# Mamba-2 blocks in a fused encoder step: the two products of x on GpSimd get a semaphore each, and one of them moves to an earlier step

## The chip, the cores and the metric

The kernel runs on 1 core of one Trainium2 chip. The metric is the device time of one launch in microseconds (us), median of several runs. Five engines work side by side and meet only through semaphores: TensorE (PE; its weight loads are PEld), VectorE (DVE), ScalarE (ACT), GpSimd (POOL) and SyncE (SP), which only issues DMAs. Each works through its own list of instructions in order: one that waits holds up all behind it on that engine.

## What is computed

One inference step of a two-layer encoder trunk for 512 prompt tokens and 64 sample tokens, in fp32: layer 0 mixes tokens by sliding-window attention, layer 1 by Mamba-2 (SSD); both have a cross-attention into 256 memory tokens, an output projection and a squared-ReLU MLP. The change lies in the SSD of layer 1:

```python
acs = jnp.cumsum(dtf * A, axis=2)
xdt = xf * dtf[..., None]
decay = jnp.exp(jnp.where(causal, diff, -jnp.inf))
cb = jnp.einsum('bcqgn,bcsgn->bcqsg', Cf, Bf)
y_diag = jnp.einsum('bcqsg,bcqsgh,bcsghp->bcqghp', cb, decay, xdt)
decay_end = jnp.exp(acs[:, :, -1:] - acs)
states = jnp.einsum('bcsgn,bcsgh,bcsghp->bcghpn', Bf, decay_end, xdt)
...
y_off = jnp.einsum('bcqgn,bcghpn,bcqgh->bcqghp', Cf, h_in, jnp.exp(acs))
```

x is needed twice: times dt (inner product, for y_diag) and times dt and the decay to the block's end (state product, for states). Then y is gated by silu(z) and normed by group.

## The kernel before

Activations lie transposed in SBUF, features on the partitions and 576 token columns (64 sample, 512 prompt) in the free dimension. Every weight matrix is cut into slabs of 1024 x 128; there are 242. A slab comes by DMA from SyncE into a ring of four (`raw`), ScalarE rounds it to fp32r (`w_hi`, L472), GpSimd makes the rest (`w_lo`, L1954), and TensorE multiplies in three products (L959). A slab is eight eighths of 6 matmuls each.

Layer 1 runs the eight SSM groups in pairs, one `turn` for each of the four pairs. `ssd_steps` (L144) writes a turn's order down once, and every engine walks the same list and does its own part of each step:

- K: an eighth of a slab of the projections for this pair's z and the next pair's x, B and C (80 eighths a turn; in the last turn z and the memory queries, 56). At a slab's end come `slab_end` and the conv on it: VectorE's `xp` (L1792, reads PSUM), ScalarE's first tap (L770), three taps on VectorE (L1807), tanh and silu (L784, L1814), and on GpSimd `w_lo` and two copies to `tails` (L2055).
- A(b), b = 0 to 4: block b (64 sample tokens, then four of 128) is transposed to tokens on partitions: `xtok`, `btok`, `cbm`.
- dec(b): ScalarE makes the decays (`dec`, L856 and L863) and the grown rows exp(acs) (`row`, L861) from rows that it fetched by DMA (L816, issued after an earlier diag, since the buffers alternate); VectorE masks dec (L1895); GpSimd multiplies the rows by C (L2095; not for block 1).
- st(b): TensorE makes the block's state from the state product (L1332); GpSimd decays the old state (`hbd`, in `rstd`, L2102).
- diag(b): TensorE makes y from dec and the inner product (L1345), and from the grown rows and the state (L1355). VectorE adds it to y (L1904) and makes the new state (L1913). GpSimd makes both products of x for block b + 1 (`scaled_x`, L2075 state product, L2076 inner product) into the buffer `xd`, which lies in `sq`.
- Q, G, N: gating on VectorE (L1918), squares on ScalarE (L870), their sums on TensorE (L1366, L1371), roots and norm (L1924).

Among the steps stand st(b), dec(b + 1), diag(b), st(b + 1) at equal distances, some 2.7 eighths in turns 1 to 3 and 1.3 in the last. `xd_done` counts after the inner product alone; st(b) waits for it, diag(b) doesn't.

## Time and profile before

| | |
|---|---|
| three runs | 1857.19, 1854.53, 1864.68 us (median 1857.19) |
| the profiled execution | 1860.35 us |
| its span, first to last instruction | 1858.5 us |
| TensorE busy | 1757.7 us, 95% |
| VectorE, ScalarE, GpSimd busy | 791.6, 698.7, 749.0 us |
| mean granted clock of TensorE | 0.986 |

The times of single instructions come from that one profiled execution. TensorE's clock has two levels, 1.2 and 2.4 GHz; a granted clock of 1.00 is the higher, 0.50 the lower. "A <- B" in a row means that A was released by B, or that tile A is made from tile B. The four turns lie between some 939 and 1284 us of the span.

### The profile page before, as it was taken

The numbers are of one execution on the slowest core, as the hardware profiler recorded it, in microseconds if no ns is written. First come the engines' busy times: TensorE is split into PE (matmuls) and PEld (weight loads), VectorE is DVE, ScalarE is ACT, GpSimd is POOL, SyncE is SP. The second block draws the span as 40 slices with busy tenths as digits, with TensorE's granted clock in tenths as the row PEclk, the third lists the DMA queues.
The fourth block names the chain that finished last, engine by engine and source line by source line (L and its number), as shares of the span: only waits on it lengthen the run. The fifth ranks groups of instructions, "written<-read, shape, count | busy, mean of one in ns | idle before, by whom it ended". The sixth has DMA issues, their size and how long they took to land.

```text
span 1858.5 us, 31140 instructions
## 1 busy us (share of the span) xinstructions
PE 1757.7 (95%) x13115; PEld 1683.0 (91%) x13115; DVE 791.6 (43%) x1534; ACT 698.7 (38%) x1318; POOL 749.0 (40%) x438
## 2 busy tenths in 40 slices
PE   6999999999999999999899999989999999999996
PEld 5997887998999999998798989877898999999996
DVE  5427777315412112126856676755504411212124
ACT  6416666324312121224455555553514312122221
POOL 1231121242736354451345555553232745445451
PEclk9999999999999999999899999998999999999998
DMA  5521210121222222221222222212121222222221
GB/s 217 191 80 52 69 64 30 57 87 51 91 84 87 80 80 85 86 80 46 84 88 87 78 94 83 92 60 102 46 80 58 91 80 80 86 85 80 80 87 67
DMA packets 47659, 153.68 MB, mean 83 GB/s; under 512 B 8257, under 2 KB 10017, under 8 KB 47265
## 3 DMA queue, kind: packets, MB, share of 16 engines
q1 hardware_dynamic: 40144, 140.59, 22.3%
q10 hardware_dynamic: 7376, 11.10, 1.8%
q8 instruction: 104, 1.70, 0.4%
q14 instruction: 35, 0.28, 0.0%
HBM read 145.21 MB, written 6.47 MB: 82 GB/s over the span
## 4 chain that ended last, share of the span: by engine, by line
PE 81%; DVE 8%; ACT 4%; POOL 3%; issue 2%; DMA 1%; SPq 0%; POOLq 0%; DVEq 0%; ACTq 0%
PE ps L959 70%; DVE mix L1459 1%; PE ps L942 1%; PE ps L1123 1%; PE ps L1094 1%; POOL sq L2075 1%; ACT dec L856 1%; DVE x L1462 1%; PE ps L1175 1%; PE ps L1112 1%; PE ps L1198 1%; PE ps L1332 1%; POOL w_lo L1954 1%; DVE big_lo L1403 1%; DMA raw<-in_slabs 1%
## 5 line engine op out<-in xcount | busy, mean ns | idle before, releaser
L1954 POOL TENSOR_TENSOR w_lo<-raw,w_hi 128x1024 fp32r<-128x1024 f32 x225 | 547.9, 2437 | 753.3 <-ACT w_hi L472 661.2
L959 PE MATMUL ps<-big_hi,w_hi 128*128 128x288 f32 x3552 | 781.1, 301 | 7.9 <-POOL w_lo L1954 3.2
L959 PE MATMUL ps<-big_lo,w_hi 128*128 128x288 f32 x3552 | 758.9, 297 | 7.7 <-DVE big_lo L1403 7.7
L959 PE MATMUL ps<-big_hi,w_lo 128*128 128x288 f32 x3552 | 765.1, 296 | 0.0
L959 PEld LDWEIGHTS ps<-big_hi,w_hi 128*128 128x128 f32 x3552 | 574.9, 190 | 17.6 <-issue 12.5
L959 PEld LDWEIGHTS ps<-big_lo,w_hi 128*128 128x128 f32 x3552 | 571.3, 189 | 13.1 <-DVE big_lo L1403 12.2
L959 PEld LDWEIGHTS ps<-big_hi,w_lo 128*128 128x128 f32 x3552 | 575.9, 189 | 0.1
L472 ACT ACTIVATE w_hi<-raw 128x1024 fp32r<-128x1024 f32 x242 | 255.3, 1057 | 489.7 <-DMA raw<-in_slabs 479.8
L1713 DVE TENSOR_TENSOR mix<-ps,mix 128x576 f32<-128x576 f32 x62 | 47.0, 758 | 307.3 <-PE ps L959 307.3
L1701 DVE SCALAR_TENSOR_TENSOR relu<-ps,rstd 128x576 f32<-128x576 f32 x60 | 45.4, 757 | 280.2 <-PE ps L959 280.2
L1997 POOL TENSOR_TENSOR hid<-relu 128x576 f32<-128x576 f32 x64 | 98.6, 1543 | 157.6 <-DVE relu L1701 157.5
L714 ACT ACTIVATE big_hi<-relu 128x576 fp32r<-128x576 f32 x64 | 43.9, 685 | 158.7 <-DVE relu L1701 157.0
L1807 DVE SCALAR_TENSOR_TENSOR u<-xp,par,u 128x579 f32<-128x579 f32 x84 | 93.2, 1110 | 7.5 <-ACT u L770 4.9
L1401 DVE TENSOR_TENSOR big_lo<-hid,big_hi 128x576 fp32r<-128x576 f32 x64 | 75.6, 1181 | 11.1 <-POOL hid L1997 11.1
L1439 DVE TENSOR_TENSOR sq_sum<-sq_sum,sq 128x576 f32<-128x576 f32 x20 | 15.1, 754 | 114.1 <-ACT sq L491 113.8
L1587 DVE CUSTOM_DVE_ANT_0 prob<-ps,bias,minus_sink 128x128 f32<-128x128 f32 (+2 forms) x120 | 48.4, 440 | 13.7 <-PE ps L1094 11.7
L959 PE MATMUL ps<-m_hi,w_hi 128*128 128x256 f32 x128 | 39.7, 310 | 15.2 <-POOL w_lo L1954 11.8
L2055 POOL COPY tails<-xp 128x3 f32<-128x3 f32 x56 | 17.3, 339 | 87.1 <-DVE xp L1792 82.0
L611 ACT ACTIVATE prob<-prob,stat 128x256 f32<-128x256 f32 (+2 forms) x108 | 50.4, 470 | 4.1 <-DVE stat L1587 4.0
L2095 POOL TENSOR_TENSOR row<-row,c_cur 128x768 f32<-128x768 f32 (+1 forms) x16 | 25.2, 1575 | 64.7 <-ACT row L861 64.7
L1605 DVE TENSOR_SCALAR prob<-prob,stat 128x256 f32<-128x256 f32 (+3 forms) x148 | 48.8, 366 | 3.0
L491 ACT ACTIVATE sq<-ps 128x576 f32<-128x576 f32 x14 | 9.1, 651 | 104.6 <-PE ps L959 104.6
(197 smaller groups left out, 1644.6 us busy)
## 6 DMA issues: line engine op xcount, KB each, us to landing
raw<-in_slabs SPq DMA_DIRECT2D x242, 512.0 KB, 3.4
row<-acs_prompt ACTq DMA_DIRECT2D x16, 384.0 KB, 3.3
bias<-in_alibi SPq DMA_DIRECT2D x12, 256.0 KB, 2.7
x<-in_x SPq DMA_DIRECT2D x2, 1152.0 KB, 8.6
out_h<-state ACTq DMA_DIRECT2D x4, 384.0 KB, 2.6
out_y<-x SPq DMA_DIRECT2D x2, 576.0 KB, 2.8
kms<-in_mk SPq DMA_DIRECT2D x2, 512.0 KB, 5.2
vms<-in_mv SPq DMA_DIRECT2D x2, 512.0 KB, 6.3
```

The costliest lines, as they stand in the source:

```text
L472: act.activation(w_hi[:, s % RING], raw[:, s % RING], ACT.Copy).then_inc(hi_done, 1)
L611: act.activation(ap, ap, ACT.Exp, bias=stat[:, r, 0, b:b + 1], scale=-1.0, accum_out=stat[:, r, 2, b:b + 1])
L714: act.activation(big_hi[:, m], relu[:, m % 2], ACT.Square).then_inc(act_hi, 1)
L959: ins = pe.matmul(ps[:, bank + h, 0:hi_c - lo_c], w[:, s % RING, kt], a[:, k0 + kt, lo_c:hi_c], start=start, stop=stop, skip_group_check=True)
L1401: ins = dve.tensor_tensor(dst, src, hi.bitcast(F32), ALU.subtract)
L1587: ins = dve.tensor_tensor_reduce(prob[half, r, k, c0:c1], ps[half, bank, k * 2 * P + c0:k * 2 * P + c1], bias[half, j, e, c0 + d:c1 + d], ...
L1605: ins = dve.tensor_scalar(ap, ap, stat[0:rows, r, 2, b:b + 1], None, ALU.mult)
L1701: dve.scalar_tensor_tensor(out=halves(relu[:, m % 2]), in0=src, scalar=0.0, in1=halves(rstd[:, 1]), op0=ALU.max, op1=ALU.mult).then_inc(fr ...
L1713: dve.tensor_tensor(halves(mix[:, m]), src, halves(mix[:, m]), ALU.add).then_inc(freed, 1)
L1807: dve.scalar_tensor_tensor(out=u[:, t], in0=xp[:, t % 2, j:j + UC], scalar=conv_par(gp, t)[:, j:j + 1], in1=u[:, t], op0=ALU.mult, op1=ALU ...
L1954: pool.tensor_tensor(w_lo[:, s % RING], raw[:, s % RING], w_hi[:, s % RING].bitcast(F32), ALU.subtract).then_inc(lo_done, 1)
L1997: pool.tensor_tensor(hid[:, m % 2], relu[:, m % 2], relu[:, m % 2], ALU.mult).then_inc(hid_done, 1)
```

## The change

The two products of x become steps of their own. The state product gets a semaphore `xs_done`, and GpSimd makes it in dec(b), ahead of the grown rows, as soon as st(b - 1) has released its half of the buffer. The inner product stays in diag(b - 1), now waits for diag(b - 1) alone, and keeps `xd_done`. TensorE's st(b) waits for `xs_done`, and diag(b) waits for `xd_done` as well.

```diff
                     elif kind == "st":
-                        pe.wait_ge(xd_done, at(loop, xd_done, b + 1))
+                        pe.wait_ge(xs_done, at(loop, xs_done, b + 1))
...
                     elif kind == "diag":
                         pe.wait_ge(decm_done, at(loop, decm_done, b + 1))
+                        pe.wait_ge(xd_done, at(loop, xd_done, b + 1))
...
-                def scaled_x(b):
+                def scaled_x(k, b, kind, done):
                     rows = DEC if b == 0 else P
+                    xb = xtok[0:rows, b].rearrange("p (h d) -> p h d", h=PH)
+                    pool.tensor_tensor(xd[0:rows, k], xb, wide(heads(kind, b)[0:rows], rows), ALU.mult).then_inc(done, 1)
+
+                def x_states(b):
+                    pool.wait_ge(xtok_done, at(loop, xtok_done, b + 1))
+                    need(pool, loop, st_done, b)
+                    alone(pool)
+                    scaled_x(1, b, 2, xs_done)
+
+                def x_within(b):
                     pool.wait_ge(xtok_done, at(loop, xtok_done, b + 1))
                     need(pool, loop, diag_done, b)
-                    need(pool, loop, st_done, b)
                     alone(pool)
-                    xb = xtok[0:rows, b].rearrange("p (h d) -> p h d", h=PH)
-                    pool.tensor_tensor(xd[0:rows, 1], xb, wide(heads(2, b)[0:rows], rows), ALU.mult)
-                    pool.tensor_tensor(xd[0:rows, 0], xb, wide(heads(0, b)[0:rows], rows), ALU.mult).then_inc(xd_done, 1)
+                    scaled_x(0, b, 0, xd_done)
...
                     elif kind == "A" and b == 1:
-                        scaled_x(0)
-                    elif kind == "dec" and b != 1:
+                        x_states(0)
+                        x_within(0)
+                    elif kind == "dec":
+                        if b:
+                            x_states(b)
+                        if b == 1:
+                            continue
                         pool.wait_ge(grown_done, at(loop, grown_done, later(b)))
...
                     elif kind == "diag" and b < BLOCKS - 1:
-                        scaled_x(b + 1)
+                        x_within(b + 1)
```

ScalarE also waits once a turn, at A(0), for `xs_done` beside `xd_done`.

GpSimd, turns 1 to 3, from the products for block 3 to the products for block 4, before (`sq` holds the products of x, `rstd` the decayed state, `row` the grown rows):

```order
L2075 TENSOR_TENSOR sq<-xtok,hs 128x384 [waits st_done,xtok_done,diag_done]
L2076 TENSOR_TENSOR sq<-xtok,hs 128x384
L2102 TENSOR_TENSOR rstd<-state,hs 128x384 [waits state_done]
L1954 TENSOR_TENSOR w_lo<-raw,w_hi 128x1024 [waits hi_done]
L2055 COPY tails<-xp 128x3 [waits freed]
L2055 COPY tails<-xp 128x3
L2095 TENSOR_TENSOR row_91<-row_91,c_cur 128x768 [waits grown_done,c_done]
L2075 TENSOR_TENSOR sq<-xtok,hs 128x384 [waits st_done,xtok_done,diag_done]
L2076 TENSOR_TENSOR sq<-xtok,hs 128x384
```

and after (the product that waits for st_done is the state product, the one that waits for diag_done the inner one):

```order
L2073 TENSOR_TENSOR sq<-xtok,hs 128x384 [waits xtok_done,diag_done]
L2116 TENSOR_TENSOR rstd<-state,hs 128x384 [waits state_done]
L1956 TENSOR_TENSOR w_lo<-raw,w_hi 128x1024 [waits hi_done]
L2057 COPY tails<-xp 128x3 [waits freed]
L2057 COPY tails<-xp 128x3
L2073 TENSOR_TENSOR sq<-xtok,hs 128x384 [waits xtok_done,st_done]
L2109 TENSOR_TENSOR row_91<-row_91,c_cur 128x768 [waits grown_done,c_done]
L2073 TENSOR_TENSOR sq<-xtok,hs 128x384 [waits xtok_done,diag_done]
```

The state product went from behind the grown rows to ahead of them; nothing else changed its place.

GpSimd in the last turn, from the first decayed state to the second, before:

```order
L2102 TENSOR_TENSOR rstd<-state,hs 128x384 [waits h_loaded,state_done]
L1954 TENSOR_TENSOR w_lo<-raw,w_hi 128x1024 [waits hi_done]
L2075 TENSOR_TENSOR sq<-xtok,hs 128x384 [waits st_done,xtok_done,diag_done]
L2076 TENSOR_TENSOR sq<-xtok,hs 128x384
L2095 TENSOR_TENSOR row_110<-row_110,c_cur 128x768 [waits grown_done,c_done]
L2075 TENSOR_TENSOR sq<-xtok,hs 128x384 [waits st_done,xtok_done,diag_done]
L2076 TENSOR_TENSOR sq<-xtok,hs 128x384
L2102 TENSOR_TENSOR rstd<-state,hs 128x384 [waits state_done]
```

and after:

```order
L2116 TENSOR_TENSOR rstd<-state,hs 128x384 [waits h_loaded,state_done]
L2073 TENSOR_TENSOR sq<-xtok,hs 128x384 [waits xtok_done,st_done]
L1956 TENSOR_TENSOR w_lo<-raw,w_hi 128x1024 [waits hi_done]
L2073 TENSOR_TENSOR sq<-xtok,hs 128x384 [waits xtok_done,diag_done]
L2073 TENSOR_TENSOR sq<-xtok,hs 128x384 [waits xtok_done,st_done]
L2109 TENSOR_TENSOR row_110<-row_110,c_cur 128x768 [waits grown_done,c_done]
L2073 TENSOR_TENSOR sq<-xtok,hs 128x384 [waits xtok_done,diag_done]
L2116 TENSOR_TENSOR rstd<-state,hs 128x384 [waits state_done]
```

Here the state product of block 1 also passes a whole w_lo.

## Rows read from the trace of the kernel before

**Rows 1.** The page, part 1: busy us of each engine (share of the span)

```profile
PE 1757.7 (95%) x13115; PEld 1683.0 (91%) x13115; DVE 791.6 (43%) x1534; ACT 698.7 (38%) x1318; POOL 749.0 (40%) x438
```

**Rows 2.** Table of waits, TensorE: total us, times, longest; whole run, first, last turn

```profile
PE ps L1332 <- POOL sq L2076: 26.7, 16, 3.8
...
PE ps L1288 <- DVE dts L1863: 4.9, 1, 4.9
...
PE ps L1332 <- POOL sq L2076: 6.0, 4, 2.4
...
PE ps L1332 <- POOL sq L2076: 9.3, 4, 3.8
PE ps L1345 <- DVE dec L1895: 0.9, 1, 0.9
```

**Rows 3.** Timeline of TensorE, first turn: start us, us, instruction [idle before <- releaser]

```profile
986.75 0.89 PE L1332 MATMUL ps<-sq,btok 128*128 128x192 f32 x4 [1.71 <-POOL sq L2076]
...
997.39 0.89 PE L1332 MATMUL ps<-sq,btok 128*128 128x192 f32 x4 [1.72 <-POOL sq L2076]
...
1011.73 2.10 PE L1366 MATMUL ps<-gsq,mats 128*128 128x288 f32 x8
```

**Rows 4.** Stretches: length, busy us of PE, PEld, DVE, ACT, POOL, clock, DMA

```profile
985.80:996.40 10.60, 8.91 (x76) 8.37 (x76) 6.96 (x11) 5.94 (x12) 7.88 (x8) 1.00 0.23 72
...
920.00:926.00 6.00, 6.00 (x23) 4.45 (x24) 5.66 (x7) 1.82 (x2) 2.99 (x3) 0.50 0.00 0
...
1156.00:1160.00 4.00, 4.00 (x18) 4.00 (x19) 1.49 (x4) 0.56 (x1) 3.29 (x3) 0.57 0.16 44
...
1236.00:1240.00 4.00, 3.98 (x15) 4.00 (x16) 1.21 (x1) 2.61 (x6) 1.69 (x1) 0.50 0.00 0
```

**Rows 5.** Timeline of GpSimd, the same block and what follows

```profile
986.57 0.82 POOL L2102 TENSOR_TENSOR rstd<-state,hs 128x384 f32<-128x384 f32 x1
987.36 2.40 POOL L1954 TENSOR_TENSOR w_lo<-raw,w_hi 128x1024 fp32r<-128x1024 f32 x1
...
993.26 1.69 POOL L2095 TENSOR_TENSOR row<-row,c_cur 128x768 f32<-128x768 f32 x1 [2.72 <-ACT row L861]
994.91 1.54 POOL L2075 TENSOR_TENSOR sq<-xtok,hs 128x384 f32<-128x384 f32 x1
...
1001.14 2.38 POOL L1954 TENSOR_TENSOR w_lo<-raw,w_hi 128x1024 fp32r<-128x1024 f32 x1
```

**Rows 6.** Timeline of VectorE, the same block and the turn's end

```profile
989.42 0.95 DVE L1814 SCALAR_TENSOR_TENSOR u<-th,u 128x579 f32<-128x579 f32 x1
990.45 2.55 DVE L1807 SCALAR_TENSOR_TENSOR u<-xp,par,u 128x579 f32<-128x579 f32 x3
993.93 1.83 DVE L1895 TENSOR_TENSOR dec<-dec,cbm 128x768 f32<-128x768 f32 x1 [0.93 <-ACT dec L863]
...
996.16 0.54 DVE L1913 TENSOR_TENSOR state<-rstd,ps 128x384 f32<-128x384 f32 x1
...
1001.08 4.77 DVE L1807 SCALAR_TENSOR_TENSOR u<-xp,par,u 128x579 f32<-128x579 f32 x3
...
1006.70 1.95 DVE L1918 TENSOR_TENSOR mix<-mix,zs 128x1728 f32<-128x1728 f32 x1
```

**Rows 7.** Timeline of ScalarE, the squares at the turn's end

```profile
1008.68 1.83 ACT L870 ACTIVATE gsq<-mix 128x576 f32<-128x576 f32 x3 [7.63 <-DVE mix L1918]
```

**Rows 8.** Timeline of the last turn, TensorE and ScalarE

```profile
1236.02 1.62 PE L1332 MATMUL ps<-sq,btok 128*128 128x192 f32 x4 [3.81 <-POOL sq L2076]
...
1253.17 1.62 PE L1332 MATMUL ps<-sq,btok 128*128 128x192 f32 x4 [3.52 <-POOL sq L2076]
...
1246.10 1.87 ACT L856 ACTIVATE dec<-row,hs 128x128 f32<-128x128 f32 x6 [7.46 <-DMA row<-acs_prompt]
```

**Rows 9.** The chain that ended last: 18 products at either level of the clock

```profile
954.36 2.37 PE ps L959 x18
...
1237.64 4.32 PE ps L959 x18
```

More of the change, by code:

```diff
@@ L380, in build @@
         dec_done, decm_done = sem("dec_done"), sem("decm_done")
-        xd_done, diag_done = sem("xd_done"), sem("diag_done")
+        xs_done, xd_done, diag_done = sem("xs_done"), sem("xd_done"), sem("diag_done")
         st_done, hbd_done, state_done = sem("st_done"), sem("hbd_done"), sem("state_done")
@@ L444, in build @@
                    "h_loaded": 16, "h_stored": 16}
-        for s_ in (tok_done, xtok_done, cbm_done, drop_done, dec_done, decm_done, xd_done, diag_done, st_done, state_done, y_done):
+        for s_ in (tok_done, xtok_done, cbm_done, drop_done, dec_done, decm_done, xs_done, xd_done, diag_done, st_done, state_done, y_done):
             SSM_PER[s_.name] = BLOCKS
@@ L833, in turn @@
                             need(act, loop, gsum_done, 0)
+                            need(act, loop, xs_done, 0)
                             need(act, loop, xd_done, 0)
```

## Prediction

> **What bounds the kernel now.** I read the page first: TensorE is busy for 95% of the span [rows 1], so only time in which it stands still, or runs at its lower clock, can be given back. The table of waits then names the place. TensorE's longest wait for another engine is the one the change aims at: the state product "st" (L1332) waits for GpSimd's second product of x (L2076), 26.7 us in 16 waits, of which 6.0 us lie in the first of the four turns and 9.3 us in the last [rows 2]. The second and third share the other 11.4 us.
>
> Next I read one block of the first turn engine by engine. st starts at 986.75 and again at 997.39, 1.71 and 1.72 us late [rows 3]: a block takes 10.6 us, of which TensorE works 8.9 us (8.91 us busy in that stretch, full clock) [rows 4]. GpSimd does six things in it: the decayed state (0.82), w_lo (2.40), two tiny copies (I count 0.2), the grown rows (1.69), and the two products of x, of the decayed state's size, the first in 1.54 [rows 5]. VectorE does a silu step (0.95), three taps (2.55), and the masking of dec (1.83), then y and the state [rows 6].
>
> The reader should see that these rows interlock. The masking is issued at 993.93, 0.67 us after the grown rows began, and takes 1.83 us; GpSimd's first product starts at 994.91, when the grown rows are over, and takes 1.54 us where the decayed state, as large, takes 0.82. Taken in turn, 994.95 to 995.76 is the masking and 995.76 to 996.45 the product. The same holds at the other end: the first tap at 1001.08 sits through a w_lo of 2.38 us, so that three taps need 4.77 us and not 2.55 [rows 5, 6]. Instructions of VectorE with both inputs in SBUF and GpSimd's instructions exclude each other; VectorE's reads of PSUM (y, state, xp) don't. So the two engines share one resource. Its load per block, without waits: GpSimd 0.82 + 2.40 + 0.2 + 1.69 + 0.82 + 0.82 = 6.7 us, VectorE 0.61 (989.76 to 990.37) + 2.55 + 0.82 = 4.0 us, together 10.7 us, less some 0.04 us at each of eight hand-overs: 10.4 us. The block has 10.6 us, and the one stretch in which neither works, 993.00 to 993.26, makes up the difference. **The wait at st is the visible end of a resource that is full in these blocks, not a mere matter of order.**
>
> **The change, part by part.** No instruction is added or removed, no DMA moves, no queue but GpSimd's gets another order. Three edits.
>
> (1) The wait of st. It no longer needs the grown rows, the masking and both products of x, only the state product, which now stands before the grown rows, in the 2.7 us for which GpSimd idles behind ScalarE (the wait named in the row at 993.26) [rows 5]. All 26.7 us of this wait are open to go, and with them what TensorE loses at its low clock after long waits.
>
> (2) The new wait. diag now waits for the inner product as well. It stands behind the grown rows, which diag needs anyway; it costs up to one product, 0.82 us, where the grown rows come last, and nothing where TensorE comes later. Queued behind it on TensorE is the whole stream of slabs.
>
> (3) The filled gap. The idle 2.7 us of GpSimd are just when VectorE runs its three taps (990.45 to 993.00) [rows 6]. Taking turns, product, taps and grown rows need the same sum as before. But the tail of the block gets worse: in the kernel before y and state (996.16 + 0.54 is the end of state) run beside a product of GpSimd; afterwards only one product is left there, and where it comes before the masking nothing is left beside y and state, since the next GpSimd instruction, the decayed state, waits for state. So the shared resource idles 0 to 1.1 us more per block; I take 0.65, the middle, for two blocks of a turn.
>
> At this point the Trainium skill can be weighed. The page "SBUF — State Buffer", section "Who interferes with whom", says that a VectorE instruction with two SBUF inputs and a GpSimd instruction that reads SBUF lock each other out for a whole instruction, and that one with an input in PSUM doesn't. The trace agrees at 994.95 and at 1001.08. By this rule the order within a block can't shorten it below 10.4 us; by durations alone GpSimd (6.7 us) and VectorE (4.0 us, and what it reads from PSUM) would each fit under TensorE's 8.9 us and the waits would vanish.
>
> Now the end of a turn. TensorE's next wait is "G", the sums over gated squares (L1366). It starts at 1011.73, and the squares it needs are done at 1008.68 + 1.83 = 1010.5: it has 1.2 us to spare [rows 3, 7]. Before the squares stands the gating (1006.70, 1.95 us) [rows 6], before that VectorE's taps, which wait for w_lo. This chain is the shared resource again. It gains nothing from the change: 1010.5 + 2 x 0.65 = 1011.8. TensorE, freed of its waits at st, would be there at 1011.73 - 5.9 = 1005.9; I find one wait left at the last st (its product comes after a w_lo, a silu step and a tap, at about 992.6, while TensorE could start at 991.2), so 1007.1. **Then it waits 4.8 us at G and starts at 1011.9**, 0.2 us later than now. The wait has moved, in one piece.
>
> A piece of that length costs more than three short ones. After the wait of 3.81 us in the last turn the granted clock is 0.50, the lower level [rows 4, 8]; st takes 1.62 us and not 0.89 and 18 products take 4.32 us and not 2.37 [rows 3, 8, 9]: 2.7 us lost. After 3.52 us st takes 1.62 us too. After the 4.9 us wait for dts the clock is 0.50 for six microseconds and more [rows 2, 4]. After the waits of 1.7 us nothing falls, and of the three of 2.4 us only the third turn's is followed by a fall (0.57 in the mean of four microseconds), about 1 us [rows 4]. I take 2.5 us per turn for G, bounds 0.8 and 4.0. Turns 1 to 3: 3 x (0.2 + 2.5) - 1.0 = **+7.1 us**.
>
> The last turn has another rhythm, four eighths of a slab between blocks and not eight, so TensorE gets to wait longer, and G follows its last diag by eight eighths, with 1.4 us of room that doesn't depend on VectorE's backlog: what is gained before the last diag stays. Its waits are 9.3 us at st and 0.9 at diag [rows 2], and low clock costs 2.7 and again some 2.5 us. Going through the blocks with the same durations: st1 no longer waits behind w_lo (3.8 us and 2.7 us of clock gained); diag2 waits 1.8 us for masking and inner product, because ScalarE's rows come by DMA only after an earlier diag (the row at 1246.10 waited 7.46 us for it [rows 8]); diag3 waits 1.1 us; st4's product comes behind w_lo and the decayed state, 3.1 us. Waits and low clock now 15.4 us, then 0.9 + 0.2 + 1.8 + 1.1 + 3.1 = 7.1 us: 8.3 us gained, less 2.7 us if the 3.1 us wait lowers the clock, which I take as likely: **-5.6 us**, bounds -9 and -3.
>
> The sum is 7.1 - 5.6 = +1.5 us on the profiled execution, 1860.35 us with its span of 1858.5 us. That lies 3.2 us above the median of the three runs, 1857.19, within their own spread of 10 us. As each of the three terms per turn could be a little smaller, I state +0.8 us: **1858.0 us**.
>
> **Rivals.** *The waits vanish.* If the exclusion is softer than I read it, or VectorE's chain isn't what G needs, all 26.7 us and the low clock of 5.2 + 1.0 us go: 1857 - 33 = 1824 us; half of it gives 1841. For it: GpSimd idles from 990.5 to 993.3. Against: the resource's sum of 10.4 us, and 1.2 us of room at G. 15%.
>
> *The last turn pays, the others break even.* If the masking gets its turn before the inner product, y and state stay covered, G starts at about 1010.6 (-1.1 us a turn) after a wait of some 3.5 us; should the clock hold there, turns 1 to 3 give -4.3 us, with the last turn's -8.3 that is -12.6: 1844.5 us; with half of the low clock 1849. 17%.
>
> *Slower.* The mechanism is the low clock at G. The place is L1366 and the products behind it, the price what the low level takes there; from 2.0 us per turn on my own sum turns from gain to loss (3 x (0.2 + 2.0) - 1.0 = 5.6). With 4.0 us per turn, 1.1 us idle in each of two blocks (+0.9 us at G over my sum) and 3 us gained in the last turn: 3 x (1.1 + 4.0) - 1.0 - 3 = +11.3 us, 1868.5 us. 10%.
>
> *The change doesn't do what it says*, since the product is still late at every st: then nothing moves, 1857. The order of GpSimd's instructions speaks against it, the last st of each turn for it. 3%.
>
> **How the numbers follow.** 55% for the forecast, 15, 17, 10 and 3% for the rivals. A measurement of this kernel can tell about 0.5% (9.3 us) from no change. Faster by more: all of the first rival, half of the second: 0.23. Slower by more: 0.08. The rest, 0.69, is within 0.5%. The range takes in the forecast with its bounds (turns 1 to 3 from -1 to +11, the last from -9 to -3: -10 to +8), the second rival's -12.6 and most of the third: 1844 to 1868 us.
>
> **What would show it.** Right: st starts with no wait in blocks 1 to 3 of turns 1 to 3, the wait table names ScalarE's squares (L870 in the kernel before) before L1366 with 3 to 5 us three times, the clock row shows 0.5 behind it, turns remain some 90 us long, and only the last turn is shorter, by 5 to 8 us; VectorE's taps take 3.3 us and more. Wrong: three taps still in 2.55 us, or L1366 starting without a wait, or turns of 84 us.

## The result, and the profile after

| | before | after |
|---|---|---|
| median of six runs | 1859.13 us | 1840.22 us |
| lowest and highest | 1848.77, 1864.68 us | 1838.10, 1845.05 us |
| ratio, 95% interval | | 0.9901 [0.9876, 0.9926] |
| the profiled execution, its span | 1860.35, 1858.5 us | 1840.2, 1838.4 us |

The changed kernel is faster by 1.0%. The forecast was 1858.0 us, with 0.69 on "within 0.5%", and a range of 1844 to 1868 us: the measured median lies below it. In a second comparison, six runs against eleven, the ratio was 0.9893 [0.9856, 0.9930].

Line numbers shift by one or two: after the change st is L1333, diag L1347 and L1357, G L1368, both products of x L2073, the grown rows L2109, the decayed state L2116, w_lo L1956, the masking L1897, the taps L1809, the gating L1920, the squares L871. First the page, part 1, as in [rows 1]:

```profile
PE 1753.9 (95%) x13115; PEld 1681.2 (91%) x13115; DVE 816.1 (44%) x1534; ACT 698.6 (38%) x1318; POOL 764.7 (42%) x438
```

VectorE and GpSimd are "busy" for 24.5 and 15.7 us more with the same instructions: time spent waiting for each other inside an instruction. Still the whole is shorter, so busy time of these two engines is no measure of the cost here.

The table of waits of TensorE (total us, times, longest), the three rows that answer to [rows 2]: the whole run first, then the last turn.

```profile
PE ps L1368 <- ACT gsq L871: 6.8, 3, 2.3
...
PE ps L1347 <- POOL sq L2073: 2.1, 1, 2.1
PE ps L1347 <- DVE dec L1897: 0.9, 1, 0.9
```

The 26.7 us of st have shrunk to three waits of 0.6 us (the timeline below shows one), and G waits three times for ScalarE's squares, as forecast, but 2.3 us each and not 4.8. Where the time went is read best from stretches of both kernels that begin and end at the same work: from the first transposition (A) of the first turn to that of the last, and from there to the last G. The columns are length, then busy us of PE, PEld, DVE, ACT, POOL, the granted clock and the DMA share. Before:

```profile
945.90:1216.60 270.70, 253.22 (x2009) 240.22 (x2008) 180.13 (x255) 151.16 (x278) 143.92 (x126) 0.99 0.26 85
1216.60:1272.90 56.30, 46.11 (x356) 42.72 (x354) 26.15 (x33) 28.42 (x63) 30.07 (x23) 0.88 0.28 98
```

After:

```profile
945.70:1206.10 260.40, 251.87 (x2010) 239.32 (x2008) 204.16 (x255) 151.31 (x279) 159.08 (x126) 0.99 0.27 89
1206.10:1251.90 45.80, 41.77 (x355) 38.93 (x353) 26.45 (x33) 28.16 (x63) 30.42 (x23) 0.96 0.35 120
```

Three turns lost 10.3 us. TensorE's idle time in them fell from 17.5 us (270.70 less 253.22) to 8.5 us, and its busy time by 1.4 us. The last turn lost 10.5 us: idle time from 10.2 to 4.0 us, busy time from 46.11 to 41.77 us, since the clock of the turn is 0.96 and not 0.88 (0.12 and 0.04 of the lengths are 6.8 and 1.8 us of lost clock). Together 20.8 us, and the spans differ by 20.1: nothing outside the SSD gained. The forecast for the three turns was +7.1 us, for the last -5.6.

One turn takes 86.3 us in the first two (89.9 before) and 87.9 in the third (90.9), where the wait at G is followed by a low clock (1180.00 to 1186.00):

```profile
1180.00:1186.00 6.00, 5.71 (x22) 3.77 (x23) 4.23 (x4) 4.59 (x7) 2.35 (x1) 0.72 0.00 0
```

Now the same block of the first turn as in [rows 3, 5 and 6]. TensorE: start us, us, instruction, and the idle time before it with its releaser.

```profile
990.98 0.89 PE L1333 MATMUL ps<-sq,btok 128*128 128x192 f32 x4 [0.57 <-POOL sq L2073]
...
1007.75 2.18 PE L1368 MATMUL ps<-gsq,mats 128*128 128x288 f32 x8 [2.27 <-ACT gsq L871]
```

GpSimd, one whole round from w_lo to w_lo:

```profile
975.80 2.92 POOL L1956 TENSOR_TENSOR w_lo<-raw,w_hi 128x1024 fp32r<-128x1024 f32 x1
978.66 0.85 POOL L2057 COPY tails<-xp 128x3 f32<-128x3 f32 x2
979.48 1.41 POOL L2073 TENSOR_TENSOR sq<-xtok,hs 128x384 f32<-128x384 f32 x1
980.86 2.20 POOL L2109 TENSOR_TENSOR row<-row,c_cur 128x768 f32<-128x768 f32 x1
983.02 1.54 POOL L2073 TENSOR_TENSOR sq<-xtok,hs 128x384 f32<-128x384 f32 x1
984.98 0.83 POOL L2116 TENSOR_TENSOR rstd<-state,hs 128x384 f32<-128x384 f32 x1 [0.42 <-DVE state L1915]
985.77 2.90 POOL L1956 TENSOR_TENSOR w_lo<-raw,w_hi 128x1024 fp32r<-128x1024 f32 x1
```

VectorE in the same round, and the gating of this turn:

```profile
975.55 0.91 DVE L1816 SCALAR_TENSOR_TENSOR u<-th,u 128x579 f32<-128x579 f32 x1
976.57 4.94 DVE L1809 SCALAR_TENSOR_TENSOR u<-xp,par,u 128x579 f32<-128x579 f32 x3
981.43 2.44 DVE L1897 TENSOR_TENSOR dec<-dec,cbm 128x768 f32<-128x768 f32 x1
983.79 0.54 DVE L1906 TENSOR_TENSOR mix<-ps,mix 128x384 f32<-128x384 f32 x1
984.26 0.54 DVE L1915 TENSOR_TENSOR state<-rstd,ps 128x384 f32<-128x384 f32 x1
...
1003.80 1.95 DVE L1920 TENSOR_TENSOR mix<-mix,zs 128x1728 f32<-128x1728 f32 x1
```

The round takes 9.97 us (975.80 to 985.77). The forecast had held 10.4 us for its floor and added 0.65. In these rows GpSimd has no idle time but 0.42 us before the decayed state, the three taps take 4.94 us (forecast: 3.3 and more), and the two engines pass the resource between them nearly all the time: this round is full, as forecast. It is only shorter than the sum said. TensorE itself was not held by it until late: its st stand 8.0, 8.7 and 9.4 us apart (964.89, 972.91, 981.58, 990.98), and only the last one waited. The gating starts at 1003.80 where it started at 1006.70 [rows 6], and so G starts at 1007.75 and not at 1011.73 [rows 3].

### The profile page after: what moved, and what is told of

Same layout as the page of the kernel before. It is cut to its first block, busy times and chain, and to the rows that moved or that the text cites. A ratio compares the mean times of both kernels' runs of the same rounds, so it can differ in the third digit from the quotient of the medians.

```text
span 1838.4 us, 31153 instructions
## 1 busy us (share of the span) xinstructions
PE 1753.9 (95%) x13115; PEld 1681.2 (91%) x13115; DVE 816.1 (44%) x1534; ACT 698.6 (38%) x1318; POOL 764.7 (42%) x438
## 4 chain that ended last, share of the span: by engine, by line
PE 80%; DVE 12%; ACT 3%; issue 3%; DMA 1%; POOL 1%; SPq 0%; DVEq 0%; ACTq 0%; POOLq 0%
PE ps L960 69%; DVE u L1809 3%; DVE mix L1461 1%; PE ps L943 1%; PE ps L1095 1%; PE ps L1124 1%; DVE x L1464 1%; PE ps L1113 1%; PE ps L1176 1%; PE ps L1199 1%; DVE big_lo L1405 1%; DMA raw<-in_slabs 1%; DVE dec L1897 1%; ACT u L770 1%; PE ps L912 1%
## 5 line engine op out<-in xcount | busy, mean ns | idle before, releaser
L1956 POOL TENSOR_TENSOR w_lo<-raw,w_hi 128x1024 fp32r<-128x1024 f32 x225 | 553.4, 2461 | 751.0 <-ACT w_hi L472 659.1
L960 PEld LDWEIGHTS ps<-big_hi,w_hi 128*128 128x128 f32 x3552 | 574.7, 190 | 17.5 <-issue 12.4
L1715 DVE TENSOR_TENSOR mix<-ps,mix 128x576 f32<-128x576 f32 x62 | 46.9, 757 | 307.2 <-PE ps L960 307.2
L1809 DVE SCALAR_TENSOR_TENSOR u<-xp,par,u 128x579 f32<-128x579 f32 x84 | 114.2, 1359 | 7.3 <-ACT u L770 4.3
L2073 POOL TENSOR_TENSOR sq<-xtok,hs 128x384 f32<-128x384 f32 (+1 forms) x40 | 48.9, 1230 | 3.3 <-ACT xtok L837 3.3
L1607 DVE TENSOR_SCALAR prob<-prob,stat 128x256 f32<-128x256 f32 (+3 forms) x148 | 48.8, 366 | 3.0
```

Source lines behind the costliest of these rows:

```text
L960: ins = pe.matmul(ps[:, bank + h, 0:hi_c - lo_c], w[:, s % RING, kt], a[:, k0 + kt, lo_c:hi_c], start=start, stop=stop, skip_group_check=True)
L1607: ins = dve.tensor_scalar(ap, ap, stat[0:rows, r, 2, b:b + 1], None, ALU.mult)
L1715: dve.tensor_tensor(halves(mix[:, m]), src, halves(mix[:, m]), ALU.add).then_inc(freed, 1)
L1809: dve.scalar_tensor_tensor(out=u[:, t], in0=xp[:, t % 2, j:j + UC], scalar=conv_par(gp, t)[:, j:j + 1], in1=u[:, t], op0=ALU.mult, op1=ALU ...
L1956: pool.tensor_tensor(w_lo[:, s % RING], raw[:, s % RING], w_hi[:, s % RING].bitcast(F32), ALU.subtract).then_inc(lo_done, 1)
L2073: pool.tensor_tensor(xd[0:rows, k], xb, wide(heads(kind, b)[0:rows], rows), ALU.mult).then_inc(done, 1)
```

## The experiments

Single runs of one kernel spread over 7 to 24 us in this study, so beside each ratio stands the length of the SSD stretch (first A to last G) in the kernel's trace. Two traces of the changed kernel have 306.3 and 306.8 us, two of the kernel with halves of w_lo 301.3 and 303.2 us; the turns repeat to 0.1 us, and what differs is the last turn. So less than 2 us of stretch says nothing by itself. Edits are against the changed kernel unless it is said otherwise.

| kernel | median us, ratio [95%] | stretch | turns 1 to 3 | last turn to G |
|---|---|---|---|---|
| before | 1857.89 to 1858.46 in the three sets | 326.9 | 89.9, 89.9, 90.9 | 56.3 |
| changed | 1840.22, 0.9901 [0.9876, 0.9926] | 306.3 | 86.3, 86.3, 87.9 | 45.8 |
| after_again, the changed kernel once more | 1836.22, 0.9893 [0.9856, 0.9930] | 306.8 | 86.3, 86.3, 87.9 | 46.3 |
| only_last_turn | 1849.03, 0.9950 [0.9924, 0.9977] | 318.6 | 91.2, 90.3, 90.0 | 47.1 |
| only_first_turns | 1847.61, 0.9942 [0.9912, 0.9972] | 314.4 | 86.2, 86.3, 87.9 | 54.0 |
| split_only | 1848.62, 0.9947 [0.9926, 0.9969] | 314.0 | 87.6, 87.6, 87.6 | 51.2 |
| move_only | 1851.47, 0.9959 [0.9934, 0.9984] | 319.4 | 88.5, 88.4, 88.4 | 54.0 |
| before_short_taps | 1858.65, one run | 326.8 | 89.9, 89.9, 91.0 | 56.1 |
| after_short_taps | 1833.90, one run | 296.3 | 82.9, 82.9, 83.4 | 47.1 |
| after_late_w_lo | 1827.36, 0.9847 [0.9805, 0.9888] | 298.5 | 84.3, 84.2, 84.3 | 45.7 |
| best | 1830.57, 0.9852 [0.9814, 0.9891] | 298.0 | 84.3, 84.3, 84.3 | 45.2 |
| after_w_lo_halves | 1823.16, one run | 301.3 | 84.8, 84.8, 84.8 | 46.9 |
| halves_again | 1827.80, 0.9834 [0.9804, 0.9865] | 303.2 | 84.8, 84.8, 84.8 | 48.8 |
| all_three | 1823.85, 0.9826 [0.9795, 0.9857] | 300.2 | 84.8, 84.8, 84.8 | 45.8 |

**The turns apart.** The new wait and the moved product in the last turn alone, and in the first three alone; here the first of them (the other has `not last`):

```diff
-                        pe.wait_ge(xs_done, at(loop, xs_done, b + 1))
+                        own = xs_done if last else xd_done
+                        pe.wait_ge(own, at(loop, own, b + 1))
...
-                        if b:
+                        if b and (last):
                             x_states(b)
...
+                        if not (last):
+                            x_states(b + 1)
                         x_within(b + 1)
```

> The change in the last turn alone; turns 1 to 3 are as before. If the two parts of the gain add up as the marks of the two traces have them (10.4 us between A and G of the last turn, 10.2 us in turns 1 to 3), this kernel is 10 us faster than before (ratio 0.9945). If the last turn's gain in the changed kernel came from a head start that the earlier turns gave it (slabs split further ahead, a shorter backlog), it is 5 us or less.

> The change in turns 1 to 3 alone. If the parts add up: 10 us faster than before (0.9945), a wait of 2.3 us at G in each of the three turns, G 3.5 us earlier per turn. By the prediction on record (turns 1 to 3 lose 7 us) it would be slower than before; if the turns' gain comes from fewer low-clock stretches it would be under 2 us with the granted clock at 1.00 throughout.

Measured: the last turn's part takes 8.3 us off the stretch and the other part 12.5 us, in sum 20.8 where the whole change takes 20.6. So the gain is not one place's, and turns 1 to 3 gain although all three waits at G are there (2.25 to 2.27 us in only_first_turns). The forecast's +7.1 us for them is refuted by this alone. The two places are not quite apart, though: only_first_turns has the last turn, whose order is that of before, in 54.0 us and not 56.3, which no run here explains. And only_last_turn needs 271.5 us for the first three and not 270.7; its clock falls in two of these turns (mean of 0.66 from 975 to 980 and from 1067 to 1072), before's in one.

**The semaphore apart from the move.** split_only leaves the state product in the step of the inner one, ahead of it, as before, but lets st wait for it alone. move_only moves the product but lets st wait for both.

```diff
-                        if b:
-                            x_states(b)
                         if b == 1:
...
+                        x_states(b + 1)
                         x_within(b + 1)
```

> Own semaphores, but the state product stays behind diag, directly ahead of the inner product; st waits for it alone. Theory of a loop of latencies (st, xp, first tap, relu, exp, grown rows, masking, product, st): the loop loses one product of 0.8 us, so some 2.5 us per turn and 3 to 5 us in the last: 10 to 12 us faster than before, the block 9.8 us long. Theory of a full shared resource (my prediction): the sum of exclusive work is the same, the block stays above 10.4 us and the gain is under 3 us.

```diff
-                        pe.wait_ge(xs_done, at(loop, xs_done, b + 1))
+                        pe.wait_ge(xd_done, at(loop, xd_done, b + 1))
```

> The state product in the earlier step, but st still waits for both products. Loop of latencies: one product leaves the loop, but it delays the taps and by them the grown rows by some 0.4 us: 3 to 6 us faster than before. Full shared resource: nothing (within 2 us). If order in GpSimd's queue alone made the gain, and not the shorter list that st waits for: 15 us or more.

Measured: the semaphore alone takes 12.9 us off the stretch (9.3 by the medians), the move alone 7.5 (6.4); together 20.4, and the change has 20.6. By its expectations a full resource would have given under 3 us and nothing. For one block (the second to the third st that waits) the timeline of TensorE in split_only shows

```profile
980.80 0.89 PE L1333 MATMUL ps<-sq,btok 128*128 128x192 f32 x4 [1.16 <-POOL sq L2073]
...
990.87 0.89 PE L1333 MATMUL ps<-sq,btok 128*128 128x192 f32 x4 [1.17 <-POOL sq L2073]
```

The block is 10.07 us long where it was 10.64 [rows 3], with the same work for all engines in the same order; G doesn't wait, and yet the turn is 2.3 us shorter. If the resource were what limits the block, a wait that ends one product earlier could not shorten it by 0.57 us. A loop of latencies can be shortened so: by a loop is meant a chain of steps on several engines, each released by the one before, that comes back to its start one block later. It lost 0.57 us and not the whole product (0.82), since the grown rows now have to wait for VectorE's taps (until 985.14 + 2.53 = 987.67) and take 1.93 us where they took 1.69 [rows 5]:

```profile
987.29 1.93 POOL L2107 TENSOR_TENSOR row<-row,c_cur 128x768 f32<-128x768 f32 x1 [1.29 <-ACT row L862]
```

**Is the resource full?** The second and third tap of each slab work on 16 of their 579 columns in the four turns (most of the conv is left out), in the kernel before and in the changed one. That takes about 1.2 us per block off the shared resource, which the expectations call the port.

```diff
+                        w = UC if j == 1 or loop.i is None else 16
-                        dve.scalar_tensor_tensor(out=u[:, t], in0=xp[:, t % 2, j:j + UC], scalar=conv_par(gp, t)[:, j:j + 1],
-                                                 in1=u[:, t], op0=ALU.mult, op1=ALU.add).then_inc(conv_done, 1)
+                        dve.scalar_tensor_tensor(out=u[:, t, 0:w], in0=xp[:, t % 2, j:j + w], scalar=conv_par(gp, t)[:, j:j + 1],
+                                                 in1=u[:, t, 0:w], op0=ALU.mult, op1=ALU.add).then_inc(conv_done, 1)
```

> The kernel before, with the second and third tap of the conv in the four turns cut to 16 of 579 columns (most of the conv is left out), so that VectorE needs 1.5 us less of the shared port in each block. Loop of latencies: the taps run beside ScalarE's relu and exp and aren't in the loop, so the blocks stay at 10.6 us, the waits at st at 1.7 us, and the stretch from the first A to the last G within 2 us of the 326.9 us of before. Full shared port (my prediction): the block falls to about 9.1 us, the waits at st to 0.3 us, the stretch to 310 us or less.

> The changed kernel with the same cut (most of the conv is left out). If the port is what holds the changed kernel's blocks and the chain before G: the wait of 2.3 us at G and of 0.6 us at the last st go, a turn lasts 84.0 us and not 86.3, the stretch from first A to last G is 297 to 300 us and not 306.3. If the chain through ScalarE holds them, G still waits over 1.5 us and the stretch is over 304 us.

Measured in the kernel before: nothing. The stretch is 326.8 us, the table of waits of TensorE and its timeline read as in [rows 2] and [rows 3] (st stands at L1332, the inner product at L2077), and VectorE's timeline shows the shorter taps followed by more idle time:

```profile
PE ps L1332 <- POOL sq L2077: 26.7, 16, 3.8
...
995.90 0.89 PE L1332 MATMUL ps<-sq,btok 128*128 128x192 f32 x4 [1.72 <-POOL sq L2077]
...
988.97 1.37 DVE L1808 SCALAR_TENSOR_TENSOR u<-xp,par,u 128x579 f32<-128x579 f32 x3
992.45 1.83 DVE L1896 TENSOR_TENSOR dec<-dec,cbm 128x768 f32<-128x768 f32 x1 [2.11 <-ACT dec L863]
```

The taps fell by 1.2 us, the idle time before the masking rose from 0.93 to 2.11 us, and the wait at st is 1.72 us as ever. **In the kernel before the resource was not what limited the block.** It was in use for nearly all of it, as the forecast had read, and yet 1.2 us more room changed nothing. What held the block was a loop of latencies through four engines (TensorE, VectorE, ScalarE, GpSimd), and its steps stand in the trace of before. ScalarE there, the same block:

```profile
989.54 0.88 ACT L770 ACTIVATE u<-xp,par 128x579 f32<-128x579 f32 x1 [4.13 <-DVE xp L1792]
990.32 1.85 ACT L856 ACTIVATE dec<-row,hs 128x128 f32<-128x128 f32 x6
992.21 0.85 ACT L861 ACTIVATE row<-row 128x768 f32<-128x768 f32 x1
```

and VectorE's xp, released by TensorE's slab end:

```profile
988.62 0.89 DVE L1792 TENSOR_TENSOR xp<-ps,rstd 128x64 f32<-128x64 f32 x3 [2.56 <-PE ps L959]
```

From st at 986.75 to the slab's end and xp at 988.62 are 1.87 us; to ScalarE's tap at 989.54, 0.92; to the decays at 990.32, 0.78; to the exponential of the rows at 992.21, 1.89; to the grown rows at 993.26, 1.05; to the first product at 994.91, 1.65; to the second at 996.42, 1.51; to the next st at 997.39, 0.97. That these steps add up to the 10.64 us of the block proves nothing, since any chain from one st to the next does. What makes them a loop is that each starts as soon as the one before lets it: the rows name the releaser, or show no idle time behind the step before on the same engine. The shared resource is in it once, where the first product takes 1.54 us and not 0.82 because the masking goes first. No run shortened one of ScalarE's steps, which would have been the direct test of the loop. The loop comes about because ScalarE takes the slab's tap ahead of the decays in its list, the slab ends only after st, and st waited for all that GpSimd does behind the grown rows. The semaphore of its own cuts the last product out of the loop (split_only); with the move as well, the grown rows and the masking are out of it too.

In the changed kernel the short taps do tell: turns of 82.9 us, and at G no wait in the first two turns and one of 0.22 us in the third. GpSimd's round, from w_lo to w_lo, falls from 9.97 to 8.5 us:

```profile
980.55 2.91 POOL L1957 TENSOR_TENSOR w_lo<-raw,w_hi 128x1024 fp32r<-128x1024 f32 x1
...
989.04 2.93 POOL L1957 TENSOR_TENSOR w_lo<-raw,w_hi 128x1024 fp32r<-128x1024 f32 x1
```

So there the resource sets the length of GpSimd's and VectorE's rounds, and through them when the last st and G can start.

**What G waits for.** In the changed kernel GpSimd makes the w_lo of the turn's last slab right behind the one before, so that the last taps go with two of them. The edit lets it wait for the gating (turns 1 to 3):

```diff
+                            if not last and b // KT == 7:
+                                pool.wait_ge(gated_done, at(loop, gated_done, 1))
                             slab_end(t if tile == "u" else None, gp + 1)
```

> The changed kernel; in turns 1 to 3 GpSimd makes the w_lo of slab_end 7 only after the gating, so that it doesn't stand in the way of the last taps before G. w_lo is some 20 us ahead of its use, so nothing waits for it. If the port before G is the limit: G no longer waits (2.3 us now), a turn lasts 84.0 us and not 86.3, the stretch from first A to last G is 299 us, and the kernel is 6 to 8 us faster than the changed one (0.986 of before). Rival: the taps are held by something else and the wait at G stays above 1.5 us.

> The changed kernel once more, on the chip of the two below: 0.990 of before (0.9876 to 0.9926), first A to last G 306 us.

Measured: the changed kernel again has 306.8 us and a ratio of 0.9893 [0.9856, 0.9930]; with the edit it is 298.5 us and 0.9847 [0.9805, 0.9888]. First the changed kernel's last taps and its w_lo, then those of the edited one with G (VectorE, GpSimd; VectorE, GpSimd, TensorE):

```profile
996.48 6.47 DVE L1809 SCALAR_TENSOR_TENSOR u<-xp,par,u 128x579 f32<-128x579 f32 x3
...
999.36 2.97 POOL L1956 TENSOR_TENSOR w_lo<-raw,w_hi 128x1024 fp32r<-128x1024 f32 x1
```

```profile
998.08 4.45 DVE L1809 SCALAR_TENSOR_TENSOR u<-xp,par,u 128x579 f32<-128x579 f32 x3
...
1005.40 2.40 POOL L1956 TENSOR_TENSOR w_lo<-raw,w_hi 128x1024 fp32r<-128x1024 f32 x1 [4.42 <-DVE mix L1920]
...
1007.33 2.18 PE L1368 MATMUL ps<-gsq,mats 128*128 128x288 f32 x8 [0.25 <-ACT gsq L871]
```

The taps fall by 2.0 us, and the wait at G by 2.0 us. This settles what the wait at G was: VectorE's backlog in its turns with w_lo, as forecast in kind. With the wait goes the low clock behind it: the third turn is 84.3 us as the others.

**The last turn's order.** The late w_lo, and in the last turn the inner product of blocks 2 to 4 in the step of the decays, ahead of the grown rows:

```diff
                         if b:
                             x_states(b)
+                            if last and b >= 2:
+                                x_within(b)
...
-                        x_within(b + 1)
+                        if not last or b == 0:
+                            x_within(b + 1)
```

> The same, and in the last turn the inner product of blocks 2 to 4 stands behind the state product in dec(b), ahead of the grown rows. There diag2 waits 2.1 us for an inner product that stands behind grown rows and masking though its buffer has been free for 2 us; 1.5 us of it should go, and 0 to 0.6 us at the next diag: 1 to 2 us faster than the kernel with late w_lo. Rival: the grown rows come later by the product and diag2 waits for them instead: within 0.5 us.

Measured: 298.0 against 298.5 us, ratios 0.9852 and 0.9847: no difference that can be told. The 1 to 2 us expected didn't come; the rival has the size, with the masking in the place of the grown rows. The wait at diag fell from 2.0 to 1.4 us and is now one for the masking, and st still waits 1.9 us. The last turn's waits in both:

```profile
PE ps L1347 <- POOL sq L2073: 2.0, 1, 2.0
PE ps L1333 <- POOL sq L2073: 1.7, 1, 1.7
```

```profile
PE ps L1347 <- DVE dec L1897: 2.3, 2, 1.4
PE ps L1333 <- POOL sq L2073: 1.9, 1, 1.9
```

**Halves of w_lo.** In the four turns each w_lo is made by two instructions of 512 columns, so that VectorE gets a turn in between:

```diff
-                pool.tensor_tensor(w_lo[:, s % RING], raw[:, s % RING], w_hi[:, s % RING].bitcast(F32), ALU.subtract).then_inc(lo_done, 1)
+                parts = ((0, KT // 2), (KT // 2, KT)) if loop.per is SSM_PER and loop.i is not None else ((0, KT),)
+                for k0, k1 in parts:
+                    ins = pool.tensor_tensor(w_lo[:, s % RING, k0:k1], raw[:, s % RING, k0:k1],
+                                             w_hi[:, s % RING, k0:k1].bitcast(F32), ALU.subtract)
+                ins.then_inc(lo_done, 1)
```

> The changed kernel with w_lo of the turns made in two halves of 512 columns. If a change of hands on the port hides an instruction's start-up (which I now think is why the block is 9.95 us long and not 10.6), more changes of hands cost nothing: the same block within 0.2 us, waits at G of 2.3 us or less. If every instruction has a fixed price on the port (384 columns 0.82 us, 768 columns 1.69, 1024 columns 2.38 us leave 0 to 0.2 us), the block is 0.2 us longer and G waits 2.5 to 3 us.

> The changed kernel with w_lo of the four turns made in two instructions of 512 columns, timed in rounds this time. Its earlier look (one run) gave 1823.2 us, but its trace lost only 5.0 us in the stretch from the first turn to the last G (301.3 us against 306.3), the rest lay behind the last turn, in work that the edit doesn't touch. Theory (gain of the stretch alone): 1840.2 - 5 = 1835 us, ratio to before 0.987, stretch 301 again, turns of 84.8 us, no wait at G and one of 1.4 us at the last st of a turn. Rival (halves help elsewhere too): 1823 us again, ratio 0.981.

> Halves of w_lo, the w_lo of a turn's last slab behind the gating, and in the last turn the inner product of blocks 2 to 4 ahead of the grown rows. Theory (the waits of a turn are alternatives: once G no longer waits, what is left at st sets the turn): turns of 83.7 to 84.8 us, stretch 297 to 299 us, no faster than the two edits without halves (298.0), ratio 0.985. Rival (the edits add up: 5.0 us by halves, 7.8 by the late w_lo, 0.5 by the last turn): stretch 293 us, ratio 0.982.

Measured: most of what the first run's 1823 us had gained did not come from the edit's place. Its stretch is 301.3 us, 5.0 less than the changed kernel's. Of its two theories neither holds whole: GpSimd's round is 10.18 us (w_lo at 978.15 and at 988.33) where it was 9.97, as the second had it, but G doesn't wait at all. In six runs the halves have 1827.80 us, between the 1835 us of the theory and the 1823 us of its rival, and 303.2 us of stretch. The turns are 84.8 us: the wait at G is gone, and one at st, now released by VectorE's state, is there instead:

```profile
PE ps L1333 <- DVE state L1915: 4.3, 3, 1.4
```

all_three has the same turns of 84.8 us, 0.5 us longer than with the late w_lo alone. The edits don't add up (its stretch of 300.2 us is nearer to the 297 to 299 of the theory than to the rival's 293). Its last turn of 45.8 us is as in the changed kernel. Its median, 1823.85 us with 0.9826 [0.9795, 0.9857], is the lowest of all, but the interval overlaps those of the late w_lo and of the halves, and by the stretch (300.2 against 298.5 us) it is not the best.

Outside the stretch the traces of the halves' kernels are also shorter, 1520.1, 1520.3 and 1517.3 us where the changed kernel and the late w_lo have 1532 us, and so is that of `best`, 1518.4, though nothing differs there between `best` and the late w_lo. The chain that ended last shows where 9.4 of these 12 to 15 us lie. Each kernel has two long series of 2832 products with no wait in them, one ahead of the SSD and one behind it. Here are both in the trace of halves_again:

```profile
473.51 368.44 PE ps L960 x2832
...
1422.48 377.85 PE ps L960 x2832
```

The granted clock is 1.00 in both. The same two lengths come back in the other traces, to 0.01 us: `best` and all_three have the short one in the first series too, after_w_lo_halves in the second, and all others have the long one twice. The traces of the kernel before and of the changed kernel have no short one, so their comparison doesn't rest on it. What makes a series short wasn't found, nor whether it is behind the spread of the runs without a trace. While that is open the three fastest kernels can't be ranked by their medians; by the turns, which have no such series in them and repeat to 0.1 us, the late w_lo and `best` (84.3 us) are ahead of the halves and of all_three (84.8).

## Why the prediction was wrong

That TensorE's wait at st is the place was right: all of the gain lies in the SSD. The forecast lost it again in what follows.

**1. "A resource that is full".** This was the step that failed: the forecast took 10.4 us as the floor of a block, because the instructions that share the resource add up to it. In the kernel before, the block was held by the loop and not by the resource (before_short_taps: 1.2 us less to share, and still 10.64 us), and once the loop was cut the round was 9.97 us. As a floor the sum was wrong too. It used eight hand-overs of 0.04 us. The rows ahead of it held the true size: the masking ended at 995.76 and the product at 996.45 [rows 5, 6], 0.69 us for an instruction that takes 0.82 alone. An instruction that has waited for the resource is over sooner after its release than it takes alone. In the round of the changed kernel: w_lo 2.26 us after the silu step's end (976.46 to 978.72) against 2.38, grown rows 1.55 after the taps' end (981.51 to 983.06) against 1.69, the inner product 0.69 after the masking's end (983.87 to 984.56) against 0.82. The first tap ends 0.62 us after w_lo (row below, read through a narrower stretch, so x1), against 0.83:

```profile
976.57 2.77 DVE L1809 SCALAR_TENSOR_TENSOR u<-xp,par,u 128x579 f32<-128x579 f32 x1
```

So a hand-over gives 0.12 to 0.21 us, and seven of them, by estimate, about 1.0 us: 10.7 less 1.0, less the tiny copies (0.2, which lie under a tap), is 9.5 us, and with 0.42 us idle 9.9 us, where the round has 9.97. The forecast's one test of fullness, that only 993.00 to 993.26 was free, counted as use the time in which VectorE's taps ran and GpSimd merely idled. That is use by one engine, but it was not what the next step waited for: the grown rows waited for ScalarE (the 2.72 us in the row at 993.26 [rows 5]).

The forecast had drawn here on the page "SBUF — State Buffer" of the Trainium skill, section "Who interferes with whom". Its rule, that such instructions lock each other out for the whole instruction, agrees with the rows above to within 0.12 to 0.21 us. The forecast's own inference from it, that the order within a block can't shorten it, didn't hold.

**2. The uncovered y and state, +0.65 us in two blocks of a turn.** It did not come about. The masking was issued at 981.43, while the inner product was held back behind the grown rows until 983.02, so the masking had its turn first, and y and the state (983.79 to 984.80) ran beside the product (983.02 to 984.56). It is what the rival "the others break even" had in it. So the w_lo of the third round starts at 995.71 and not at 997.99 (1.3 us of it from two rounds of 9.97 us for 10.64, 0.9 us from what lies ahead of them), and this makes 2.3 of the 2.9 us by which the gating came earlier, where the forecast had it later. GpSimd before, then after:

```profile
997.99 2.40 POOL L1954 TENSOR_TENSOR w_lo<-raw,w_hi 128x1024 fp32r<-128x1024 f32 x1
```

```profile
995.71 2.89 POOL L1956 TENSOR_TENSOR w_lo<-raw,w_hi 128x1024 fp32r<-128x1024 f32 x1
```

**3. "The wait has moved, in one piece".** Right in kind: G waited for the squares in all three turns. Wrong in size, 2.27 us for 4.8, since the squares ended at 1007.6 (row below, 1005.78 + 1.83) and not at 1011.8, and TensorE was there 1.6 us earlier too (1007.75 less 2.27 is 1005.48, forecast 1007.1; the wait at the last st was 0.57 and not 1.2, where the forecast's own 992.6 less 991.2 would have been 1.4). The low clock forecast at 2.5 us a turn came once in three, in the third, at 1.6 us (87.9 less 86.3). ScalarE, after:

```profile
1005.78 1.83 ACT L871 ACTIVATE gsq<-mix 128x576 f32<-128x576 f32 x3 [9.33 <-DVE mix L1920]
```

**4. The last turn.** Forecast -5.6 us with bounds -9 and -3, measured -10.5. st1 no longer waits behind w_lo, and diag2 waits (forecast 1.8 us, measured 2.14): both right. The waits of 1.1 us at diag3 and of 3.1 us at st4, with a low clock behind it, didn't come. Timeline of TensorE, last turn, and the stretch around the wait:

```profile
1231.17 0.88 PE L1347 MATMUL ps<-dec,sq 128*64 128x128 f32 x12 [2.14 <-POOL sq L2073]
...
1238.24 0.88 PE L1347 MATMUL ps<-dec,sq 128*64 128x128 f32 x12
...
1240.87 0.89 PE L1333 MATMUL ps<-sq,btok 128*128 128x192 f32 x4
...
1230.00:1238.00 8.00, 6.83 (x51) 6.52 (x52) 5.69 (x8) 6.65 (x16) 7.58 (x6) 0.79 0.14 51
```

TensorE came to them late, after the wait of 2.14 us and the low clock behind it (0.79 in the mean of 1230 to 1238). In the kernels whose clock holds there, st4 does wait: 1.7 us in after_late_w_lo, 1.9 in best, though diag waits there as well (2.0 and 1.4 us). So the place was right and the 3.1 us were too many, and the sum took no account of the low clock behind the first wait, whose time is given back where TensorE would have waited later.

**Of what the forecast named as signs of error**, "turns of 84 us" was the nearest; they came at 86.3, and at 84.3 once G's backlog was taken away. The rival "the waits vanish, half of it" (1841 us) has the time by coincidence: the waits at st went almost whole (26.7 to 1.7 us), and G and diag took back 8.9 us (6.8 and 2.1). The one on y and state has part of the mechanism. Neither has the loop.

## What to carry to other kernels

When a block's period equals a sum of busy times, test the other explanation before believing in a full resource. Follow one round back from releaser to releaser, and see whether it is a loop that closes without a free step. Then take some load off the resource: here 1.2 us less left the block of before at 10.64 us, and took 1.5 us off the round of the changed kernel, where the resource really was full. A semaphore that let TensorE go on after the one product it needed paid 12.9 us, moving that product off the loop another 7.5. After such a change look for the next backlog's owner (here the w_lo that shared with the last taps); holding one instruction back until the late chain is through gave 8 us more.

## What the runs showed of the hardware

An instruction of VectorE or GpSimd that has to wait for the other engine ends 0.12 to 0.21 us sooner after its release than its duration alone: tap 0.62 for 0.83, product 0.69 for 0.82, grown rows 1.55 for 1.69, w_lo 2.26 for 2.38. So alternating instructions on the two engines need less than the sum of their durations, by an estimated 1.0 us in a block of 10 us. That the waiting instruction does its start-up in the meantime would explain it; no run separates that out.

Of two waiters, the one that was issued first had the next turn in the block above (masking at 981.43 before the product at 983.02). It isn't so everywhere: in the kernel before, a tap issued at 1001.08 sat through a whole w_lo issued at 1001.14 [rows 5, 6].

Waits of 2.27 us at G left the clock at 1.00 in two turns (the first is in the row below), and one of the same length in the third was followed by 0.72 in the mean of six microseconds.

```profile
1005.00:1020.00 15.00, 12.73 (x87) 11.35 (x86) 10.15 (x15) 12.84 (x16) 5.33 (x6) 1.00 0.19 63
```

Series of 2832 products with no wait in them took 377.85 us or 368.44 us, both at a granted clock of 1.00 and both in one trace of one kernel (halves_again).
